# Norm and mix of the differential attention rewritten, and five steps reordered, in a four-layer two-block kernel

## The reference

```python
# diff_attention: 4 heads, two score maps each, causal
pr = softmax(s, axis=-1)
a = pr[:, :, 0] - lam * pr[:, :, 1]
ya = a @ v
lam = exp(sum(lp[0] * lp[1])) - exp(sum(lp[2] * lp[3])) + lam_init
ya = rms_norm(ya, subln_g) * (1.0 - lam_init)     # x * rsqrt(mean(x*x) + 1e-5) * g
# dsa_attention: 8 heads, an index score picks 64 keys of each query, softmax over them, @ v
# causal_attention (mla, moba): 8 heads, softmax(q @ k * scale) @ v
# retention: 4 heads, decayed q @ k without softmax, @ v, then a group norm
```

## Time and profile before

| | |
|---|---|
| time of the profiled execution | 1855.59 us |
| its span | 1853.7 us |
| median of three timed runs | 1854.09 us |
| busy: PE, DVE, ACT, POOL | 97%, 62%, 46%, 4% |
| chain that ended last: PE, DVE, ACT | 80%, 14%, 4% |
| projections and attention, first layer | 0 to 190 us |
| experts, first layer | 265 to 480 us |
| attention, second layer of the first block | 495 to 680 us |
| second block | 985 to 1854 us |

### The profile page before, as it was taken

The page is one execution under the profiler, slowest core; times in us unless marked ns, Lnnn a source line. Parts: engine busy times, 40 slices in busy tenths (PEclk is TensorE's granted clock), DMA queues, the critical chain, the costliest instruction groups (busy, mean ns, idle before and its releaser), DMA issues.

```text
span 1853.7 us, 28789 instructions
## 1 busy us (share of the span) xinstructions
PE 1791.8 (97%) x11812; PEld 1453.5 (78%) x11812; DVE 1141.8 (62%) x2106; ACT 859.2 (46%) x1508; POOL 66.1 (4%) x76
## 2 busy tenths in 40 slices
PE   9999999999899999999989999999999999999998
PEld 7789885555678899555548899988888889988887
DVE  6876773233678867433248666775557577675554
ACT  5555542232545444323225565355555555345554
POOL 1000000000000000000001000000101000000001
PEclk9999999999999999999999999999999999999999
DMA  8426669999643475999985434445554533355552
GB/s 307 148 90 262 224 252 414 421 420 420 238 179 115 147 316 205 353 421 421 420 351 171 159 114 151 155 173 185 201 183 156 204 129 123 137 185 189 194 185 88
DMA packets 61050, 426.59 MB, mean 230 GB/s; under 512 B 6960, under 2 KB 7104, under 8 KB 11888
## 3 DMA queue, kind: packets, MB, share of 16 engines
q1 hardware_dynamic: 59760, 421.65, 60.1%
q0 software_dynamic: 432, 1.82, 0.3%
q10 hardware_dynamic: 720, 1.19, 0.2%
HBM read 423.59 MB, written 1.05 MB: 229 GB/s over the span
## 4 chain that ended last, share of the span: by engine, by line
PE 80%; DVE 14%; ACT 4%; issue 1%; POOL 1%; DMA 0%; DVEq 0%; POOLq 0%; ACTq 0%
PE bank L1153 63%; PE scp L1153 14%; DVE WSl L1548 5%; ACT SC L2235 1%; PE bank L1418 1%; ACT WSh L2177 1%; DVE sm L1706 1%; POOL sm L2438 1%; PE bank L1304 1%; PE bank L1277 1%; PE bank L1251 1%; DVE sm L1501 1%; DVE XB L1815 1%; DVE scp L1704 0%; DVE TMP L1691 0%
## 5 line engine op out<-in xcount | busy, mean ns | idle before, releaser
L1548 DVE TENSOR_TENSOR WSl<-ring,WSh 128x1024 fp32r<-128x1024 f32 (+4 forms) x404 | 462.6, 1188 | 153.8 <-ACT WSh L2177 153.4
L2177 ACT CAST WSh<-ring 128x1024 fp32r<-128x1024 f32 (+4 forms) x404 | 390.5, 1020 | 147.8 <-PE scp L1153 80.1
L1153 PE MATMUL bank<-XB,WSh 128*128 128x256 f32 (+1 forms) x1920 | 433.5, 314 | 4.3 <-DVE GT L1830 2.5
L1153 PE MATMUL bank<-XB,WSl 128*128 128x256 f32 x1216 | 331.8, 281 | 0.0
L1153 PEld LDWEIGHTS bank<-XB,WSh 128*128 128x128 f32 x1920 | 311.1, 191 | 24.1 <-DVE WSl L1548 4.2
L1153 PE MATMUL bank<-WSh,XB 128*128 128x512 f32 (+4 forms) x1088 | 313.6, 368 | 5.2 <-DVE WSl L1548 3.5
L1153 PEld LDWEIGHTS bank<-XB,WSl 128*128 128x128 f32 x1216 | 231.4, 190 | 6.5 <-DVE XB L1815 0.6
L1153 PEld LDWEIGHTS bank<-WSh,XB 128*128 128x128 f32 x1088 | 199.5, 189 | 36.1 <-DVE WSl L1548 4.9
L1153 PE MATMUL bank<-WSl,XB 128*128 128x512 f32 (+4 forms) x544 | 198.9, 366 | 0.0
L2047 DVE SCALAR_TENSOR_TENSOR TMP<-TMP,bank 128x128 f32<-128x128 f32 x64 | 18.4, 288 | 279.0 <-ACT TMP L2365 279.0
L1153 PE MATMUL scp<-WSh,FA 128*128 128x512 f32 x512 | 159.1, 389 | 0.0
(11 more groups left out here) (315 smaller groups left out, 2486.1 us busy)
## 6 DMA issues: line engine op xcount, KB each, us to landing
ring<-wts SPq DMA_DIRECT2D x222, 1024.0 KB, 4.8
A<-wts SPq DMA_DIRECT2D x64, 1024.0 KB, 14.5
V<-wts SPq DMA_DIRECT2D x30, 1024.0 KB, 15.7
WSF<-wts SPq DMA_DIRECT2D x24, 1024.0 KB, 16.2
SC<-wts SPq DMA_DIRECT2D x16, 1024.0 KB, 15.5
PT<-wts SPq DMA_DIRECT2D x14, 1024.0 KB, 16.7
H<-wts SPq DMA_DIRECT2D x12, 1024.0 KB, 16.2
ring<-wts SPq DMA_DIRECT2D x8, 584.0 KB, 5.2
```

Source lines behind the costliest of these rows:

```text
L1153: return nc.tensor.matmul(dst, lhsT, rhs, start=start, stop=stop)
L1548: nc.vector.tensor_tensor(lo[:, c], buf[:, c], hi[:, c].bitcast(F32), ALU.subtract).then_inc(*lo_done.inc(("block", i)))
L2177: nc.scalar.copy(hi[:, c], buffers[s.buffer][:, c]).then_inc(*hi_done.inc(("half", i, k)))
```

## The change

1. `mix` leaves the first map undivided. It takes the reciprocal of the second sum only, w = z0 * lambda / z1 for four heads, and for each head one instruction x0 = x1 * w + x0. A last instruction stores z0 * z0 * eps / (1 - lam_init)^2 for the norm.
2. The norm of diff and of retention takes its statistics from the bank and writes `O` from the bank; there is no copy in front. For diff one instruction scales all four heads, with the factor 1 - lam_init taken into the variance. The bank is released by these last instructions.
3. In `attend` the scores of tile 1 are two steps of four heads, one in front of `turn_p` of tile 0 and one behind.
4. The scores of dsa's tile 0 stand in front of diff's last `weighted`.
5. The todo list is ga0, ga1, sv0, sv1, ga2, ga3. With the same `fill` counts, sv0 and sv1 come where ga2 and ga3 were, and ga2 and ga3 where sv0 and sv1 were.
6. The turns IT stand in front of `lambda`.

```diff
-    def attend(self, att, l, heads, fills, between=None, pre=0):
-        scp, p = self.use("scp", "act"), self.use("P", "pe")
-        self.add("scores", name=att, l=l, t=0, scp=scp)
+    def attend(self, att, l, heads, fills, between=None, pre=0, scored=None, then=None):
+        if scored is None:
+            scored = self.use("scp", "act")
+            self.add("scores", name=att, l=l, t=0, scp=scored)
+        scp, p = scored, self.use("P", "pe")
...
-        self.add("scores", name=att, l=l, t=1, scp=scp)
+        self.add("scores", name=att, l=l, t=1, scp=scp, c=0)
         self.turn_p(att, l, 0, heads, p)
+        self.add("scores", name=att, l=l, t=1, scp=scp, c=1)
...
         self.fill(fills[2])
+        if then is not None:
+            then()
         self.add("weighted", name=att, l=l, t=1, u=self.bank(evict), pt=self.now("PT"), o=o)
...
+        self.turn("IT", l, 10, P)
         self.add("lambda", l=l, u=self.bank("dve"))
-        self.turn("IT", l, 10, P)
...
-        self.todo.extend(self.gates("w_in", l, "ga", W1["ga"], src))
-        self.todo.extend(self.wide("w_in", "sv", l, 0, W1["sv"], 512, src))
+        gates = self.gates("w_in", l, "ga", W1["ga"], src)
+        self.todo.extend([*gates[:2], *self.wide("w_in", "sv", l, 0, W1["sv"], 512, src), *gates[2:]])
...
-        self.attend("diff", l, 4, (1, 2, 0))
+        ahead = []
+
+        def dsa_scores():
+            ahead.append(self.use("scp", "act"))
+            self.add("scores", name="dsa", l=l, t=0, scp=ahead[0])
+        self.attend("diff", l, 4, (1, 2, 0), then=dsa_scores)
...
-        self.attend("dsa", l, 8, (1, 2, 1), diff_out, pre=1)
+        self.attend("dsa", l, 8, (1, 2, 1), diff_out, pre=1, scored=ahead[0])
```

```diff
 # TensorE, scores
-                    for h in range(heads):
+                    for h in range(heads) if s.c is None else range(4 * s.c, 4 * s.c + 4):
 # VectorE, norm_stats, at its end
+                if even is not None:
+                    var4 = sm[:, base:base + 2 * groups].rearrange("p (a b c) -> p a b c", a=2, c=2)[:, :, :, 1]
+                    nc.vector.scalar_tensor_tensor(var4, var4, 1.0 / even ** 2, eps, ALU.mult, ALU.add).then_inc(*dve_done.inc(("var", *name)))
+                else:
+                    nc.vector.tensor_scalar(var, var, eps, None, ALU.add).then_inc(*dve_done.inc(("var", *name)))
 # VectorE, mix
-                    nc.vector.reciprocal(rz, zs[t]).then_inc(*dve_done.inc())
-                    dve.wait_ge(dve_done)
-                    nc.vector.tensor_scalar(w1, rz, lam, None, ALU.mult).then_inc(*dve_done.inc())
+                    nc.vector.reciprocal(rz, z1).then_inc(*dve_done.inc())
+                    dve.wait_ge(dve_done)
+                    nc.vector.scalar_tensor_tensor(w, z0, lam, rz, ALU.mult, ALU.mult).then_inc(*dve_done.inc())
                     dve.wait_ge(dve_done)
                     for h in range(4):
...
-                        nc.vector.tensor_scalar(x1, x1, w1[:, p1:p1 + 1], None, ALU.mult).then_inc(*dve_done.inc())
-                        dve.wait_ge(dve_done)
-                        nc.vector.scalar_tensor_tensor(x0_, x0_, rz[:, p0:p0 + 1], x1, ALU.mult, ALU.add).then_inc(
+                        nc.vector.scalar_tensor_tensor(x0_, x1, sm[:, 56 + h:57 + h], x0_, ALU.mult, ALU.add).then_inc(
                             *dve_done.inc(("mixed", l, t, h)))
+                    nc.vector.scalar_tensor_tensor(ez, z0, LN_EPS / even ** 2, z0, ALU.mult, ALU.mult).then_inc(*dve_done.inc())
 # VectorE, weighted of diff and ret
-                        nc.vector.tensor_copy(ob, bank[u % 4][:, :].rearrange("p (h d) -> p h d", h=4)).then_inc(*dve_done.inc(("bank", u)))
...
+                        mean, var = norm_stats(b4, 4, P, 64, ez, True, None, name, 1.0 - (0.8 - 0.6 * math.exp(-0.3 * l)))
+                        dve.wait_ge(pool_done, "pow", *name)
+                        nc.vector.tensor_tensor(ob, b4, var.unsqueeze(2).broadcast_to([P, 4, P]), ALU.mult).then_inc(
+                            *dve_done.inc(("bank", u), name))
+                    else:
+                        mean, var = norm_stats(b4, 4, P, 64, GN_EPS, False, None, name)
...
+                            nc.vector.tensor_scalar(ob[:, h, :], b4[:, h, :], mean[:, h:h + 1], var[:, h:h + 1],
+                                                    ALU.subtract, ALU.mult).then_inc(*dve_done.inc(("bank", u), name))
```

More of the change, by code:

```diff
@@ L1490, in vector_program, with norm_stats @@
             index_n, route_n, tmp_used = {}, {}, 0
-            def norm_stats(src, groups, n, base, eps, rms, parts, name):
+            def norm_stats(src, groups, n, base, eps, rms, parts, name, even=None):
                 chunk = min(n, 512)
@@ L1515, in norm_stats @@
                     dve.wait_ge(dve_done)
-                nc.vector.tensor_scalar(var, var, eps, None, ALU.add).then_inc(*dve_done.inc(("var", *name)))
+                if even is not None:
[3 more added lines that the diff above has]
+                    nc.vector.tensor_scalar(var, var, eps, None, ALU.add).then_inc(*dve_done.inc(("var", *name)))
                 return mean, var
@@ L1720, in vector_program @@
                 elif s.kind == "mix":
-                    kl, w1, rz = P * (t + 1), sm[:, 56:64], rzs[t]
+                    kl, w = P * (t + 1), sm[:, 56:60].rearrange("p (a b) -> p a b", a=2)
+                    (z0, z1), (ez, rz) = ([v.rearrange("p (a c b) -> p a c b", a=2, c=2)[:, :, c, :] for c in range(2)] for v in (zs[t], rzs[t]))
+                    even = 1.0 - (0.8 - 0.6 * math.exp(-0.3 * l))
                     dve.wait_ge(act_done, "exp", "diff", l, t, 1)
-                    nc.vector.reciprocal(rz, zs[t]).then_inc(*dve_done.inc())
+                    nc.vector.reciprocal(rz, z1).then_inc(*dve_done.inc())
                     dve.wait_ge(dve_done)
-                    nc.vector.tensor_scalar(w1, rz, lam, None, ALU.mult).then_inc(*dve_done.inc())
+                    nc.vector.scalar_tensor_tensor(w, z0, lam, rz, ALU.mult, ALU.mult).then_inc(*dve_done.inc())
                     dve.wait_ge(dve_done)
                     for h in range(4):
-                        p0, p1 = pos_of(2 * h), pos_of(2 * h + 1)
-                        x1, x0_ = SC[:, p1, 0:kl], SC[:, p0, 0:kl]
-                        nc.vector.tensor_scalar(x1, x1, w1[:, p1:p1 + 1], None, ALU.mult).then_inc(*dve_done.inc())
-                        dve.wait_ge(dve_done)
-                        nc.vector.scalar_tensor_tensor(x0_, x0_, rz[:, p0:p0 + 1], x1, ALU.mult, ALU.add).then_inc(
+                        x0_, x1 = (SC[:, pos_of(2 * h + c), 0:kl] for c in range(2))
+                        nc.vector.scalar_tensor_tensor(x0_, x1, sm[:, 56 + h:57 + h], x0_, ALU.mult, ALU.add).then_inc(
                             *dve_done.inc(("mixed", l, t, h)))
+                    nc.vector.scalar_tensor_tensor(ez, z0, LN_EPS / even ** 2, z0, ALU.mult, ALU.mult).then_inc(*dve_done.inc())
                 elif s.kind == "decay":
@@ L1762, in vector_program @@
                     dve.wait_ge(freed("O", s.o - 1), "O", s.o - 1)
-                    if s.name in ("diff", "ret"):
-                        ob = OB[t]
-                        nc.vector.tensor_copy(ob, bank[u % 4][:, :].rearrange("p (h d) -> p h d", h=4)).then_inc(*dve_done.inc(("bank", u)))
-                        dve.wait_ge(dve_done)
-                        name = ("weighted", s.name, l, t)
-                        rms = s.name == "diff"
-                        mean, var = norm_stats(ob, 4, P, 64, LN_EPS if rms else GN_EPS, rms, None, name)
+                    ob, b4 = OB[t], bank[u % 4][:, :].rearrange("p (h d) -> p h d", h=4)
+                    name = ("weighted", s.name, l, t)
+                    if s.name == "diff":
+                        ez = rzs[t].rearrange("p (a c b) -> p a c b", a=2, c=2)[:, :, 0, :]
+                        mean, var = norm_stats(b4, 4, P, 64, ez, True, None, name, 1.0 - (0.8 - 0.6 * math.exp(-0.3 * l)))
[4 more added lines that the diff above has]
+                        mean, var = norm_stats(b4, 4, P, 64, GN_EPS, False, None, name)
                         dve.wait_ge(pool_done, "pow", *name)
                         for h in range(4):
-                            if rms:
-                                nc.vector.tensor_scalar(ob[:, h, :], ob[:, h, :], var[:, h:h + 1],
-                                                        1.0 - (0.8 - 0.6 * math.exp(-0.3 * l)), ALU.mult, ALU.mult).then_inc(*dve_done.inc(name))
-                            else:
-                                nc.vector.tensor_scalar(ob[:, h, :], ob[:, h, :], mean[:, h:h + 1], var[:, h:h + 1],
-                                                        ALU.subtract, ALU.mult).then_inc(*dve_done.inc(name))
+                            nc.vector.tensor_scalar(ob[:, h, :], b4[:, h, :], mean[:, h:h + 1], var[:, h:h + 1],
+                                                    ALU.subtract, ALU.mult).then_inc(*dve_done.inc(("bank", u), name))
```

## The result

In four runs the kernel after took 1834.95 us (median; 1833.96 to 1835.69), the kernel before in the same comparison 1853.51 (1852.72 to 1854.83). The ratio of the two is 0.9889, with an interval of 0.9856 to 0.9921: the kernel after takes less time, a gain of about 1% that is clear of noise, 18.6 us by the medians and some 20.6 by the ratio (14.6 to 26.7). The forecast was 1839.3, with 1834.5 to 1846.0 as its range. The median itself lies just inside the lower end; the ratio applied to the 1854.1 of before gives 1833.5, just outside. The change gives more than was forecast.

A forecast was written before the change was run, and what follows sets the result against it. TensorE, busy 1791.8 of 1853.7 us, was taken as the bound, through its standstills and low clock. Gains of 3.4, 9.4 and 5.4 us sum to 18.2; less 3.4 for a clock fall, 14.8: 1854.1 to 1839.3 us, range 1834.5 to 1846.

The forecast's parts named there:

- Part 1: Turns IT in front of lambda: TensorE's waits there shrink by 2.1 us in the first layer, 1.3 in the second; -3.4.
- Second block: Mla, moba and retention in both layers: 4.5 us from scores in two parts, 0.9 from retention's norm; together -5.4 us.
- Part 3: Scores of t=1 split around t=0's transposes: removes 0.68 us for diff, 0.8 to 0.9 for mla and moba per layer.
- The waits: TensorE's waits in each layer's first block, forecast gone: 0.68 + 0.87 + 0.82 + 1.92 + 0.83 = 5.1 us.
- the clock: In dsa, behind new waits of about 2.4 us: the clock falls in one of two layers, +3.4 us.
- the 4.7 us of the first block: Gain per layer from diff to dsa: waits gone 5.1, clock 3.4, less new waits of 1.4 and 2.4 us.
- what is late next: VectorE in dsa: product t=0 waits 1.4 us, t=1's transposes some 2.4; the stage ends at 156.2 instead of 160.86.
- VectorE's lead: VectorE's queue at the copy for dsa's t=0 product comes 3.6 us earlier and no more, its casts standing behind oa.
- Reading the bank: Retention's norm: four multiplications from the bank give back at most 4 x 0.1 of the copy's 0.68 us.
- The clock falls in neither layer: Rival, chance 0.15: no fall of the clock behind dsa's new waits in either layer, 1836 us.
- VectorE takes it back: Rival, chance 0.12: VectorE comes no earlier in dsa, the new wait eats the gains there; 1845.3 us.
- The bank held longer: Rival, chance 0.03: diff t=1's second transposes wait for t=0's bank if mix and norm are not shorter; 1857 us.

The follow-up runs named there:

- part 1 alone: The kernel before with only the turns IT moved in front of lambda: 1851.93 us against 1854.85, ratio 0.9984.
- part 2: Undone: the kernel after with the old mix and old norm (items 1 and 2 reversed): 1844.96 us against 1854.85, ratio 0.9946.
- part 3: Undone: the kernel after with the scores of t=1 in one step in front of the transposes: 1841.35 us against 1854.85, ratio 0.9930.
- part 4: Undone: the kernel after with dsa's first scores again behind diff's last product: 1833.86 us against 1855.16, ratio 0.9888.
- part 5: Undone: the kernel after with sv again behind the gates ga2 and ga3: 1834.01 us against 1854.56, ratio 0.9893.

## Why the prediction was wrong, step by step

Right were the direction, the places, and the sizes of most terms. These sizes held:

- *Part 1*, -3.4: 3.14 in the profiled pair, 3.4 in the trace of part 1 alone (2.9 by its medians).
- *Second block*, -5.4: 5.87. Part 3 has 4.9 of it instead of 4.5, the retention 0.97 instead of 0.9.
- *The waits.* Four of the five in a layer went as told. Of the fifth, in front of dsa's product, 0.82 us are left, where 1.4 were forecast. The new wait for the branch addition came, with 1.38 and 1.28 us instead of 2.4; with the small gaps around it, it holds TensorE up for 2.0 and 1.7 us.

**The step that failed is the clock: "I take it that the clock falls after them in one of the two layers: +3.4".** It fell in neither. The term was wrong in two ways. First, the new wait was set against the 2.75 us of waits at 139.5 as "a little shorter", but it is 1.38 us long. The wait for the branch addition comes up in 18 stretches of these profiles, with 0.96 to 1.39 us, and behind none of them does the clock fall. Second, the price: the 3.4 us that the sum credits each layer for a fall mended, and takes over for the new one, are 2.80 us on TensorE and 0.8 to 0.9 in the stage. What a fall behind the new wait would have cost, no run shows. Without the term the sum is 18.2 and the forecast 1835.9 us, within 1 us of the median.

Against the profiled pair the account is this: from 14.8 us forecast to 21.5 found, the clock term is 3.4, the first block 1.5 (10.9 instead of 9.4), the second block 0.5, part 1 -0.3, and 1.6 are the fall in the routing, which is luck.

A second error does not show in the number: *how the 4.7 us of the first block come about*. The sum credits TensorE's waits (5.1) and its clock (3.4), and charges 3.8 for VectorE. The experiments turn that around. With TensorE's waits and clock mended and VectorE as before, 0.8 to 0.9 us are won in a layer; with VectorE's work alone mended 3.9 to 4.3. Undone one by one from the kernel after, in the two layers: part 2 4.6 and 4.6, part 3 0.4 and 0.5, part 4 0.0 and 0.1, part 5 0.4 and 0.6. The forecast's own paragraph on what is late next had this: the gate starts when VectorE lets it. The sum for the first block came out nearly right because it carried that limit to the end, not because its terms were the causes.

**VectorE's lead was 4.6 us, not 3.6.** Its copy for dsa went from 142.76 to 136.04, and 2.13 of that came with the start of the stage. The timeline of VectorE, first two rows of the kernel before (the start and the end of mix t=1), then the mix and norm of diff and that copy in the kernel after:

```profile
113.62 0.20 DVE L1723 RECIPROCAL sm<-sm 128x8 f32<-128x8 f32 x1 [2.00 <-ACT SC L2235]
...
117.28 0.68 DVE L1765 COPY O<-bank 128x512 f32<-128x512 f32 x1
```

```profile
110.23 0.18 DVE L1739 RECIPROCAL sm<-sm 128x4 f32<-128x4 f32 x1 [2.00 <-ACT SC L2248]
...
110.70 1.67 DVE L1745 SCALAR_TENSOR_TENSOR SC<-SC,sm 128x256 f32<-128x256 f32 x4
...
112.36 0.88 DVE L1511 BATCH_NORM_STATS2 sm<-bank 128x6 f32<-128x128 f32 x4
...
115.49 0.69 DVE L1783 TENSOR_TENSOR O<-bank,sm 128x512 f32<-128x512 f32 x1 [1.23 <-POOL sm L2451]
116.10 4.62 DVE L1562 TENSOR_TENSOR WSl<-ring,WSh 128x1024 fp32r<-128x1024 f32 x4
...
136.04 0.68 DVE L1767 COPY PT<-bank 128x512 f32<-128x512 f32 x1
```

Mix t=1 lasts 2.13 us to the next instruction (3.66 before, from 113.62 to 117.28), mix t=0 1.61 (2.85), the norm of t=0 3.74 (4.63), that of t=1 3.63 (4.53). So 1.24 + 1.53 + 0.89 + 0.90 = 4.56, by prices that the forecast had (1.1, 1.4, 0.9, 0.9) and cut to 3.6 on the ground that VectorE's casts stand behind oa on ScalarE; ScalarE's queue came earlier with it, and there is no wait in front of VectorE's two low parts ahead of that copy (at 129.93 and 133.78 us). That is 1 us a layer, and the measured stretch is 5.4 to 5.5 instead of 4.7.

**Reading the bank.** The forecast allowed at most 0.1 us for each of retention's four multiplications. Before and after, on VectorE:

```profile
1167.07 1.12 DVE L1776 TENSOR_SCALAR O<-O,sm 128x128 f32<-128x128 f32 x4 [1.13 <-POOL sm L2438]
```

```profile
1148.17 1.37 DVE L1789 TENSOR_SCALAR O<-bank,sm 128x128 f32<-128x128 f32 x4 [1.13 <-POOL sm L2451]
```

Each went from 342 ns out of SBUF to 402 out of the bank, so the four give back 0.25 of the copy's 0.68 us. What is left, 0.43, agrees with the 0.49 that the stage is shorter. The Trainium skill, "VectorE: DVE Perf Modes", section "Why PSUM operands drop a tier", says that fp32 runs at the single rate as soon as an operand lies in PSUM. The trace agrees for this operation: 128 columns more cost 136 ns out of the bank (402 to the 538 of the earlier trace rows) and 67 ns out of SBUF (282 to 349). The statistics cost nearly the same from both (0.87 and 0.88 us for four).

**The rivals.** "The clock falls in neither layer" had 0.15 and 1836 us: it was the case that came. "VectorE takes it back" was right in that VectorE sets the end, and wrong in its condition, that VectorE does not come earlier. "The bank held longer" needs mix as long as before; tried, it costs 5.7 us against the kernel after, not enough to be slower than before.

## What to carry to other kernels

When TensorE is busy 97% and a stage still has waits on it, follow the stage to its end and ask whose instruction frees the last buffer. Here it was VectorE's, so a microsecond less on VectorE was a microsecond less of the stage, while waits removed ahead of that point, and even a mended clock, came back for the most part as another wait. In the second block, where TensorE sets the end, the removed waits were worth about their length. To judge parts worth less than the scatter of the runs, compare the length of a stage between two fixed instructions in each trace, and note beside it whether the clock fell there.

## What the runs showed of the hardware

A fall of the clock does not follow from the waits in the kernel alone. With 1.92 and 0.83 us of waits before and behind the transposes it fell for 6.8 us in the first layer of the kernel before and not at all in that of the kernel with part 1. With one wait of 2.57 or 2.66 us it fell in one layer and not in the other. Over the 28 stretches of the first block in the 14 profiles: in the 12 that have a wait of TensorE of 1.70 us or more it fell in 7, in the 16 whose longest wait is 1.39 us or less it fell in none. But the fall in the routing of 5 profiles has only a wait of 0.47 us close in front of it. What decides it stays open. A term like "+3.4 if it falls" needs a chance, not a decision.

And its price depends on the place. The Trainium skill, "TensorE: Matmul & The Clock Gate", section "Terms", puts the penalty at the throttled time times the lost share of the clock. For the 3.4 us in the routing, where TensorE had no wait in which to hide them, that is 1.7, and the trace shows 1.6. For the 6.8 us in dsa it is 3.4; TensorE itself is 2.80 us late at the next transposes, and the stretches show 0.8 to 0.9. For a fall of 3.4 us in the first block it is 1.7: nothing is to be seen of it in the kernel that copies the bank first, and 1.0 us in the one with the old mix, where it comes earlier in the stage. So in these traces the product is an upper bound, a little above what TensorE loses, and in a stage whose end another engine sets well above what the stage loses.
